# Moving 32 of a decoder layer's expert dot products from one stage to the next, with new layouts for two scratch tensors

## The chip, the cores and the metric

One core of a Trainium2 chip runs the whole kernel. The metric is the device time of one execution in microseconds (us), median of several runs. Five engines work side by side: TensorE (PE: matrix products), VectorE (DVE), ScalarE (ACT), GpSimd (POOL) and SyncE (SP, which here only issues transfers). They meet through semaphores. Transfers issued by SP share one queue, fetches of rows by index are issued by POOL on another; the same 16 transfer engines serve both.

## What is computed

The kernel is one layer of a decoder trunk for 512 tokens of 1024 channels; the change touches its last part, the PEER expert mixer with 16384 experts of one neuron each:

```python
def peer_ffn(h, w_q, sub_keys, u_experts, v_experts):
    ...                       # queries, scores, top 16 of each of 8 heads
    idx = ...                 # (tokens, 8, 16): 128 experts for each token
    g = jax.nn.softmax(best_s, axis=-1)
    act = jax.nn.gelu(jnp.einsum('cd,chkd->chk', xc, u_experts[ic]), approximate=False)
    wgt = gc * act
    return jnp.einsum('chk,chkd->cd', wgt, v_experts[ic])
```

The result is x + gate2 * peer_ffn(h2), followed by a last RMS norm.

## The kernel before

The expert mixer does not fetch rows for 384 of the 512 tokens. It computes the activation of all 16384 experts for them with TensorE, in 128 tiles of 128 experts (`phase_experts`), each with 24 matmuls in split precision: operands are cut into a high part (ACT) and a low part (POOL here), and three products are summed. The Gelu of each tile (ACT, L1647) goes to a DRAM tensor `acts`, two tiles at a time (`store`). Tiles 0 to 79 are "plain": DVE transposes their rows (L1714). Tiles 80 to 127 are "gated": their rows were turned in earlier stages and are loaded from DRAM (`load_turned`, L1594); beside them a dense table of gates for tokens and experts is built from one-hot products (DVE L1838 and L1842, 24 small matmuls of PE, ACT's copies L1685) and stored in 12 chunks of 32 tokens, 2 MB each (`gates_out`, L1589), one for every four tiles.

The first 128 tokens take the other way, by fetched rows. For each of their 128 choices (`NSLOT`) POOL fetches one row of `u_experts` for each token, 128 rows of 1024 channels (`fetch`, L1314), and DVE multiplies it with h, held in PSUM as `p_h`, and sums (`dot`, L1701). There are 4 buffers (`RING`). Which tile each dot stands beside is written out by hand: `dots_by(t)` puts 56 before tile 80 and the other 72 in the 48 gated tiles; `rows_by(t)` lets POOL run 4 ahead. On POOL the fetches stand behind the low part of each tile (L1857).

`phase_combine` multiplies activations with gates and with `v_experts`, in 32 groups of 4 tiles (`GT`), 72 matmuls of 512 columns each. For each group SP loads the activations (`at`, 768 KB), the gates (`gt`, 768 KB) and four tiles of values (`v`, 512 KB each, one buffer each, loaded again when its low part is done). DVE multiplies activations with gates (L2052, or L2074 in four pieces for group 0), takes low parts of values (L2046) and weights (L2057), ACT takes high parts (L2019, L2023). Between groups DVE adds fetched rows of `v_experts` for the first 128 tokens (`add_row`, L2067), 128 over 31 groups (`adds_by`), with 8 buffers (`VRING`). Each stage is a block; a block begins when all engines and the awaited stores of the last one are done. The values of group 0 and its activations are loaded before the end of `phase_experts`, its gates at the start of `phase_combine`.

Of the kernel before, what the change touches and what calls it, by code (L numbers as in the profile page):

```python
# [1316 lines left out]
def expert_groups(a, acts):  # L1317

    return a["v_experts"][0].rearrange("(g x p) d -> g p x d", x=GT, p=P), acts.rearrange("(g x) p t -> g p x t", x=GT)
# [192 lines left out]

def rows_by(t):

    return 0 if t < KNOWN_AT else min(NSLOT, dots_by(t + 1 if t + 1 < PLAIN else t) + RING)


def phase_experts(nc, a, keep, scores, top, topi, acts, gates, turned, raw, u_in, v, at0, v_in, w_in0, rows, few):

    with ExitStack() as stack:  # L1520
# [13 lines left out]
        gs = [k.sb(f"gs{j}", [P, P, CH]) for j in range(2)]  # L1534
        end = k.at
# [19 lines left out]
        iota = k.sb("iota", [P, P], BF16)  # L1555
        assert k.at <= TOP_AT
        k.at = TOP_AT
        parts = k.sb("parts", [P, NT // GTOK, 3, GTOK, 2], BF16)
        assert k.at <= V_AT
# [9 lines left out]
        au = acts.rearrange("(b x) p t -> b p x t", x=2)  # L1569
# [8 lines left out]
        def _(sp):  # L1578
# [4 lines left out]
            def store(n, j):  # L1583
                sp.wait_ge(sem["act_ok"], 2 * n + 2)
                sp.dma_start(au[n], ao[j][:, :, :]).then_inc(sem[f"a_out{j}"], 16)
# [10 lines left out]
            with sp.Fori(0, PLAIN // 4 - 1) as i:  # L1596
                for j in range(2):
                    load(2 * i + j + 2, j)
                    store(2 * i + j, j)
            for j in range(2):  # L1600
                sp.wait_ge(sem["ut_ok"], PLAIN - 2 + 2 * j)
                load_turned(j, j)
                store(PLAIN // 2 - 2 + j, j)

            def turn(i, last=False):
                for x in range(UNROLL // 2):
# [6 lines left out]
                    store(n, x % 2)  # L1613
                    if last and x == UNROLL // 2 - 2:
# [79 lines left out]
        def _(dve):  # L1694
# [108 lines left out]
            assert tile[0] <= SOFT_AT + 2  # L1803
            for t in range(tile[0], SOFT_AT + 2):
# [127 lines left out]

def adds_by(g):

    return NSLOT * g // (NE // P // GT - 1)


def phase_combine(nc, a, keep, acts, gates, gate2_row, x2, out, v, at0, v_in, w_in0, rows, few):

    with ExitStack() as stack:  # L1940
# [3 lines left out]
        at1 = k.sb("at1", [P, GT, NT])  # L1944
        at = [at0, at1]
        gt = [k.sb(f"gt{j}", [P, CHUNKS, GT * CH]) for j in range(2)]
        ssq, fin, root = (k.sb(n, [P, TT]) for n in ("ssq", "fin", "root"))
        assert k.at <= AT0_AT
        k.at = Y_AT + 48 * KB
        w_hi = [k.sb(f"w_hi{j}", [P, GT, NT], F32R) for j in range(2)]  # L1950
        w_lo = [k.sb(f"w_lo{j}", [P, GT, NT], F32R) for j in range(2)]
        gate2 = k.sb("gate2", [P, D])
        g_fin = k.sb("g_fin", [P, D])
# [12 lines left out]
        names = ("w_in1 w0_ok hi0_ok gf_in vhi_ok vlo_ok w_ok whi_ok wlo_ok mm "  # L1966
# [7 lines left out]
        gv = gates.rearrange("c j (g x) t -> g j c (x t)", x=GT)  # L1974
# [3 lines left out]
        def _(sp):  # L1978
# [5 lines left out]
            def weights(g, j):  # L1984
                sp.dma_start(at[j][:, :, :], av[g]).then_inc(sem[f"w_in{j}"], 16)
                sp.dma_start(gt[j][:, :, :], gv[g]).then_inc(sem[f"w_in{j}"], 16)
# [18 lines left out]
        def _(pool):  # L2005
            for n in range(NSLOT):
                if n >= VRING:
                    pool.wait_ge(sem["add_ok"], n - VRING + 1)
                gather_rows(nc, ring[n % VRING], a["v_experts"], few["idx"], n).then_inc(row_in[n % VRING], 16)

        @block.scalar
        def _(act):
# [16 lines left out]
            nc.scalar.activation(few["dots"][:, :], few["dots"][:, :], ACT.Gelu).then_inc(sem["dg_ok"], 1)  # L2029
            split(1, 1, True)  # L2030
            weights(1, 1)
            with act.Fori(1, NG // 2) as i:
# [9 lines left out]
        def _(dve):  # L2042
# [5 lines left out]
            def weigh(g):  # L2048
                j = g % 2
                dve.wait_ge(sem[f"w_in{j}"], 32 * (g // 2) + 32)  # L2050
                x = at[j][:, :, :].rearrange("p x (c t) -> p x c t", t=CH)
                nc.vector.tensor_tensor(x, x, gt[j][:, :, :].rearrange("p c (x t) -> p x c t", t=CH), ALU.mult).then_inc(sem["w_ok"], 1)  # L2052
# [6 lines left out]
            def add_row(n):  # L2059

                dve.wait_ge(row_in[n % VRING], 16 * (n // VRING) + 16)
                w = few["wg"][:, n:n + 1]
                if n == 0:
                    nc.vector.tensor_scalar(p_a[:, :], ring[0], w, None, ALU.mult).then_inc(sem["add_ok"], 1)
# [175 lines left out]
```

## Time and profile before

| what | value |
|---|---|
| median of 3 runs | 2024.35 us (2022.98 to 2035.23) |
| the profiled execution, its own time | 2025.17 us |
| its span, first to last instruction | 2023.3 us |
| PE / DVE / ACT / POOL busy | 1868 / 1498 / 721 / 781 us |
| expert tiles, last matmul | 1469.2 us |
| combine, first matmul | 1487.2 us |
| mean granted TensorE clock | 0.965 |

The span is the time from the first to the last instruction of the profiled execution; 1.9 us of its own time lie outside. Busy time is a share of the whole kernel and says little of a stage: a stage has to be read from windows, and its end from what the engines wait for. PEclk is the share of full clock (2.4 GHz) that TensorE was granted, DMA share the mean busy share of the 16 transfer engines as the profile counts it (it can come out above 1), GB/s what they moved.

### The profile page before, as it was taken

The numbers are of one execution on the slowest core, as the hardware profiler recorded it, in microseconds if no ns is written. First come the engines' busy times: TensorE is split into PE (matmuls) and PEld (weight loads), VectorE is DVE, ScalarE is ACT, GpSimd is POOL, SyncE is SP. The second block draws the span as 40 slices with busy tenths as digits, with TensorE's granted clock in tenths as the row PEclk, the third lists the DMA queues.
The fourth block names the chain that finished last, engine by engine and source line by source line (L and its number), as shares of the span: only waits on it lengthen the run. The fifth ranks groups of instructions, "written<-read, shape, count | busy, mean of one in ns | idle before, by whom it ended". The sixth has DMA issues, their size and how long they took to land. (4 is left out here: it accounts for less than half of the span.)

```text
span 2023.3 us, 28278 instructions
## 1 busy us (share of the span) xinstructions
PE 1868.2 (92%) x10096; PEld 1632.8 (81%) x10096; DVE 1497.6 (74%) x2260; ACT 720.6 (36%) x969; POOL 780.8 (39%) x487
## 2 busy tenths in 40 slices
PE   4999979999898799989999998999969999999997
PEld 4788757777777688989999988898858888888886
DVE  6566377774446488999895688888858887888887
ACT  3222234444323222323333354555533333333331
POOL 0000096000041001568787787888622332322320
PEclk7999989999999899999999999999979999999999
DMA  8799288878582431669999989999999999999991
GB/s 294 239 334 319 93 214 225 242 215 244 170 277 42 93 77 35 157 177 268 294 268 287 270 256 311 313 316 319 331 361 381 383 384 366 363 355 354 362 352 64
DMA packets 325795, 526.33 MB, mean 260 GB/s; under 512 B 20266, under 2 KB 243291, under 8 KB 321116
## 3 DMA queue, kind: packets, MB, share of 16 engines
q1 hardware_dynamic: 288860, 391.23, 64.2%
q0 software_dynamic: 36864, 134.23, 19.4%
q8 instruction: 34, 0.56, 0.1%
q14 instruction: 37, 0.30, 0.0%
HBM read 438.88 MB, written 85.99 MB: 259 GB/s over the span
## 5 line engine op out<-in xcount | busy, mean ns | idle before, releaser
L123 PE MATMUL u_s<-h_hi,u_hi 128*128 128x384 f32 x1024 | 358.1, 350 | 46.3 <-POOL u_lo L1857 41.6
L124 PE MATMUL u_s<-h_lo,u_hi 128*128 128x384 f32 x1024 | 348.8, 341 | 0.0
L125 PE MATMUL u_s<-h_hi,u_lo 128*128 128x384 f32 x1024 | 348.8, 341 | 0.0
L123 PE MATMUL v_o<-v_v_hi,v_w_hi 128*128 128x512 f32 x768 | 299.9, 391 | 18.7 <-DVE v_w_lo L2080 18.0
L124 PE MATMUL v_o<-v_v_lo,v_w_hi 128*128 128x512 f32 x768 | 299.7, 390 | 0.0
L125 PE MATMUL v_o<-v_v_hi,v_w_lo 128*128 128x512 f32 x768 | 299.5, 390 | 0.0
L2019 ACT ACTIVATE v_v_hi<-v_raw 128x1024 fp32r<-128x1024 f32 x128 | 127.7, 1053 | 340.0 <-PE v_o L125 268.3
L123 PEld LDWEIGHTS u_s<-h_hi,u_hi 128*128 128x128 f32 x1024 | 197.0, 192 | 59.6 <-POOL u_lo L1857 39.4
L1857 POOL TENSOR_TENSOR u_lo<-u_ut,u_hi 128x1024 fp32r<-128x1024 f32 x79 | 198.4, 2511 | 89.2 <-ACT u_hi L1635 89.1
L2046 DVE TENSOR_TENSOR v_v_lo<-v_raw,v_v_hi 128x1024 fp32r<-128x1024 f32 x128 | 149.4, 1221 | 87.8 <-ACT v_v_hi L2019 87.5
L124 PEld LDWEIGHTS u_s<-h_lo,u_hi 128*128 128x128 f32 x1024 | 197.2, 193 | 0.0
L125 PEld LDWEIGHTS u_s<-h_hi,u_lo 128*128 128x128 f32 x1024 | 197.0, 192 | 0.0
L1701 DVE CUSTOM_DVE_ANT_0 rows_buf<-rows_buf,u_h 128x1024 f32<-128x1024 f32 x128 | 154.2, 1210 | 45.8 <-DMA rows_buf<-in_u_experts_dram,few_idx 45.6
L123 PEld LDWEIGHTS v_o<-v_v_hi,v_w_hi 128*128 128x128 f32 x768 | 144.7, 188 | 49.4 <-issue 19.4
L1314 POOL DMA_INDIRECT rows_buf<-in_u_experts_dram,few_idx x128 | 169.2, 1322 | 36.3 <-DVE few_dots L1701 16.6
L1647 ACT ACTIVATE u_ao<-u_s 128x384 f32<-128x384 f32 x128 | 63.3, 494 | 326.7 <-PE u_s L125 309.5
L125 PEld LDWEIGHTS v_o<-v_v_hi,v_w_lo 128*128 128x128 f32 x768 | 144.7, 188 | 30.3
L124 PEld LDWEIGHTS v_o<-v_v_lo,v_w_hi 128*128 128x128 f32 x768 | 144.7, 188 | 30.0
L1314 POOL DMA_INDIRECT rows_buf<-in_v_experts_dram,few_idx x64 | 80.7, 1261 | 185.6 <-DVE v_a L2067 148.5
L1857 POOL TENSOR_TENSOR u_lo<-u_raw,u_hi 128x1024 fp32r<-128x1024 f32 x48 | 136.0, 2834 | 39.7 <-ACT u_hi L1640 39.0
L1314 POOL DMA_INDIRECT v_acc<-in_v_experts_dram,few_idx x64 | 78.4, 1225 | 167.4 <-DVE v_a L2067 164.4
L1714 DVE STREAM_TRANSPOSE u_ut<-u_raw 128x1024 f32<-128x1024 f32 x80 | 99.4, 1242 | 47.9 <-DMA u_raw<-in_u_experts_dram 47.5
(313 smaller groups left out, 3803.0 us busy)
## 6 DMA issues: line engine op xcount, KB each, us to landing
v_raw<-in_v_experts_dram SPq DMA_DIRECT2D x128, 512.0 KB
u_raw<-in_u_experts_dram SPq DMA_DIRECT2D x160, 256.0 KB
expert_acts<-u_ao SPq DMA_DIRECT2D x64, 384.0 KB
u_raw<-turned_experts SPq DMA_DIRECT2D x96, 256.0 KB
expert_gates<-u_gs SPq DMA_DIRECT2D x12, 2048.0 KB, 12.0
v_gt<-expert_gates SPq DMA_DIRECT2D x32, 768.0 KB
w_in_raw<-in_w_in_dram SPq DMA_DIRECT2D x17, 1024.0 KB, 11.7
proj_ada<-in_w_ada_dram SPq DMA_DIRECT2D x8, 2048.0 KB, 13.1
```

What stands on the lines that cost most here:

```text
L123: nc.tensor.matmul(out, w[0], x[0], start=first, stop=False)
L124: nc.tensor.matmul(out, w[0], x[1], start=False, stop=False)
L125: return nc.tensor.matmul(out, w[1], x[0], start=False, stop=last)
L1314: return nc.gpsimd.indirect_dma_start(to, None, table[0], bass.IndirectOffsetOnAxis(idx[:, n:n + 1], 0))
L1647: nc.scalar.activation(ao[j // 2][:, j % 2, :], p_s[j % 2][:, 0:NT], ACT.Gelu).then_inc(sem["act_ok"], 1)
L1701: nc.vector.tensor_tensor_reduce(out=row, in0=row, in1=p_h[:, :], scale=1.0, scalar=0.0, op0=ALU.mult, op1=ALU.add, accum_out=few["dots"][ ...
L1714: nc.vector.transpose(ut[j % 2][:, :, :].rearrange("p m (b e) -> p b m e", b=4), half.rearrange("p b (m r) -> p b m r", m=KD)).then_inc(se ...
L1857: nc.gpsimd.tensor_tensor(lo[j][:, :, :], ut[j][:, :, :] if t < PLAIN else at_half(t % 4), hi[j][:, :, :].bitcast(F32), ALU.subtract).then ...
L2019: nc.scalar.activation(v_hi[j][:, x, :], v[:, x, :], ACT.Copy).then_inc(sem["vhi_ok"], 1)
L2046: nc.vector.tensor_tensor(v_lo[g % 2][:, x, :], v[:, x, :], v_hi[g % 2][:, x, :].bitcast(F32), ALU.subtract).then_inc(sem["vlo_ok"], 1)
```

## The change

- `dots_by` puts 46 dots into the plain tiles and 50 into the gated ones (`SOON`, 96 in all). The other 32 (`LATE`) are done in the combine: two a group in groups 1 to 16, ahead of the rows of `v_experts`. All 160 row steps are spread evenly over the 31 groups. For them h is copied from PSUM to SBUF (`ht`) at the end of the plain tiles, and ACT does a second Gelu after group 17, whose product with the gates DVE takes after group 19.
- `acts` is laid out as [32 groups, 128, 4, 384] instead of [128 tiles, 128, 384]. The stores are still of two tiles; a load of a group is one contiguous piece in each partition.
- Gates are loaded for two groups at a time from group 2 on (`gate_pair`), pieces of 1024 bytes instead of 512, and up to two groups ahead.
- The first group's gates are loaded at the end of `phase_experts`, eleven of twelve chunks (`gt0`); the twelfth is read where it was computed (`gs[1]`). Its multiplication is in eight pieces instead of four.
- The first two tiles of group 0's values are loaded as soon as their buffer is free, and not with the other two. `g_fin` and `gate2`, used at the end, are loaded at the end instead of behind group 1. Some buffers change place for this; SP's and ACT's loops are written out or split.

```diff
-    ... acts.rearrange("(g x) p t -> g x p t", x=GT)
+    ... acts
-DOTS_FROM, EARLY_DOTS = 22, 56
+DOTS_FROM, EARLY_DOTS = 22, 46
+LATE = 32
+SOON = NSLOT - LATE
+LATE_BY = 16
...
-    return EARLY_DOTS + (NSLOT - EARLY_DOTS) * (t + 1 - PLAIN) // GATED
+    return EARLY_DOTS + (SOON - EARLY_DOTS) * (t + 1 - PLAIN) // GATED
...
+def gates_of(gates, n):
+
+    return gates.rearrange("c j (g x) t -> g j c (x t)", x=n)
...
                         sp.dma_start(at0[:, :, :], av[0]).then_inc(w_in0, 16)
-                        sp.wait_ge(sem["lo_ok"], TILES)
+                        for y in range(2):
+                            sp.wait_ge(sem[f"g_out{y}"], 16 * (TURNS - y))
+                        sp.dma_start(gt0[:, 0:CHUNKS - 1, :], gates_of(gates, GT)[0][:, 0:CHUNKS - 1, :]).then_inc(w_in0, 16)
                         for y in range(GT):
+                            if y % 2 == 0:
+                                sp.wait_ge(sem["lo_ok"], TILES - 2 + y)
                             sp.dma_start(v[:, y, :], vv[0][:, y, :]).then_inc(v_in[y], 16)
...
+            dve.wait_ge(sem["ht_ok"], 2)
+            dve.wait_ge(steps.sem, steps.n)
+            nc.vector.tensor_copy(ht[:, :], p_h[:, :])
...
+def late_by(g):
+
+    return LATE * min(g, LATE_BY) // LATE_BY
...
-    return NSLOT * g // (NE // P // GT - 1)
+    return (NSLOT + LATE) * g // (NE // P // GT - 1) - late_by(g)
...
-            sp.dma_start(gt[0][:, :, :], gv[0]).then_inc(sem["w_in0"], 16)
-            weights(1, 1)
+            def gate_pair(i):
+                sp.dma_start(gt[i % 2][:, :, :, :].rearrange("p c y n -> p c (y n)"), gv[i]).then_inc(sem[f"gt_in{i % 2}"], 16)
+
+            sp.dma_start(gt[0][:, :, 1, :], gv1).then_inc(sem["gt_in0"], 16)
+            weights(1)
             values(1)
+            gate_pair(1)
+            for g in range(2, NG):
+                if g % 2 == 0 and g + 2 < NG:
+                    sp.wait_ge(sem["w_ok"], g - 1)
+                    gate_pair(g // 2 + 1)
+                sp.wait_ge(sem["wlo_ok"], g - 1)
+                weights(g)
+                values(g)
+            sp.wait_ge(sem["w_ok"], NG - 3)
             sp.dma_start(g_fin[:, :], ...)
             sp.dma_start(gate2[:, :], ...)
-            with sp.Fori(1, NG // 2) as i:
-                for j in range(2):
-                    sp.wait_ge(sem["wlo_ok"], 2 * i + j - 1)
-                    weights(2 * i + j, j)
-                    values(2 * i + j)
...
+            act.wait_ge(sem["add_ok"], LATE + adds_by(LATE_BY - 1))
+            nc.scalar.activation(few["dots"][:, SOON:], few["dots"][:, SOON:], ACT.Gelu).then_inc(sem["dg_ok"], 1)
...
+            def late_dot(at_row, n):
+
+                dve.wait_ge(row_in[at_row % VRING], 16 * (at_row // VRING) + 16)
+                row = ring[at_row % VRING]
+                nc.vector.tensor_tensor_reduce(out=row, in0=row, in1=ht[:, :], scale=1.0, scalar=0.0, op0=ALU.mult, op1=ALU.add,
+                                               accum_out=few["dots"][:, late_slot(n):late_slot(n) + 1]).then_inc(sem["add_ok"], 1)
...
-                    o = at[0][:, x, :].rearrange("p (c t) -> p c t", t=CH)
-                    nc.vector.tensor_tensor(o, o, gt[0][:, :, x * CH:(x + 1) * CH], ALU.mult).then_inc(sem["w0_ok"], 1)
+                    o = at[0][:, x, 0:NT - CH].rearrange("p (c t) -> p c t", t=CH)
+                    nc.vector.tensor_tensor(o, o, gt0[:, 0:CHUNKS - 1, x * CH:(x + 1) * CH], ALU.mult)
+                    o = at[0][:, x, NT - CH:]
+                    nc.vector.tensor_tensor(o, o, gs[1][:, x, :], ALU.mult).then_inc(sem["w0_ok"], 1)
...
                 if g == 1:
                     dve.wait_ge(sem["wg_ok"], 1)
+                for n in range(late_by(g - 1), late_by(g)):
+                    late_dot(at_row, n)
+                    at_row += 1
                 for n in range(adds_by(g - 1), adds_by(g)):
-                    add_row(n)
+                    add_row(at_row, n)
+                    at_row += 1
+                if g == LATE_BY + 3:
+                    dve.wait_ge(sem["dg_ok"], 2)
+                    nc.vector.tensor_tensor(few["wg"][:, SOON:], few["dots"][:, SOON:], sel[:, 2, 0, SOON:], ALU.mult).then_inc(sem["wg_ok"], 1)
+                    dve.wait_ge(sem["wg_ok"], 2)
...
-        acts = nc.dram_tensor("expert_acts", [NE // P, P, NT], F32, kind="Internal").ap()
+        acts = nc.dram_tensor("expert_acts", [NE // P // GT, P, GT, NT], F32, kind="Internal").ap()
```

## Rows read from the trace of the kernel before

**Rows 1.** Windows: length, busy times, PEclk, DMA share, GB/s

```profile
891.00:1165.00 274.00, 261.13 (x1458) 252.16 (x1458) 220.94 (x496) 92.13 (x125) 211.46 (x121) 0.99 1.02 273
1165.00:1205.00 40.00, 40.00 (x348) 38.65 (x348) 36.82 (x36) 23.10 (x27) 36.49 (x17) 1.00 0.87 258
1205.00:1469.00 264.00, 239.58 (x1959) 231.29 (x1956) 214.05 (x202) 137.66 (x163) 202.56 (x99) 0.95 1.03 317
1520.00:1600.00 80.00, 80.00 (x354) 66.24 (x354) 70.39 (x54) 29.06 (x26) 25.64 (x21) 1.00 1.06 380
1700.00:1900.00 200.00, 200.00 (x884) 165.60 (x883) 160.06 (x124) 64.69 (x62) 64.02 (x51) 1.00 1.01 359
```

**Rows 2.** Timeline of ACT: start, length, instruction, idle before and its releaser

```profile
1268.23 0.49 ACT L1647 ACTIVATE u_ao<-u_s 128x384 f32<-128x384 f32 x1 [1.48 <-PE u_s L125]
...
1284.97 0.49 ACT L1647 ACTIVATE u_ao<-u_s 128x384 f32<-128x384 f32 x1 [2.17 <-PE u_s L125]
...
1294.17 0.53 ACT L1647 ACTIVATE u_ao<-u_s 128x384 f32<-128x384 f32 x1
```

**Rows 3.** Waits from 1165 to 1470 us: total, times, longest

```profile
DVE rows_buf L1701 <- DMA rows_buf<-in_u_experts_dram,few_idx: 45.6, 27, 4.7
ACT u_hi L1640 <- DMA u_raw<-turned_experts: 44.9, 12, 6.5
...
PE u_s L123 <- POOL u_lo L1857: 23.0, 8, 7.0
```

**Rows 4.** Windows of two microseconds in the gated tiles, same columns

```profile
1264.00:1266.00 2.00, 2.00 (x13) 2.00 (x13) 1.97 (x3) 2.00 (x3) 1.99 (x2) 1.00 1.00 208
1276.00:1278.00 2.00, 2.00 (x14) 2.00 (x13) 1.48 (x1) 1.40 (x2) 1.98 (x2) 1.00 1.04 442
```

**Rows 5.** Timeline of DVE, steady part of the combine

```profile
1764.57 1.75 DVE L2052 TENSOR_TENSOR at_raw<-at_raw,v_gt 128x1536 f32<-128x1536 f32 x1
1769.31 4.63 DVE L2046 TENSOR_TENSOR v_v_lo<-v_raw,v_v_hi 128x1024 fp32r<-128x1024 f32 x4 [2.98 <-ACT v_v_hi L2019]
...
1775.52 2.68 DVE L2067 SCALAR_TENSOR_TENSOR v_a<-v_acc,few_wg,v_a 128x1024 f32<-128x1024 f32 x2
...
1780.89 1.75 DVE L2052 TENSOR_TENSOR v_at<-v_at,v_gt 128x1536 f32<-128x1536 f32 x1
```

**Rows 6.** Timeline of DVE and of ACT, early in the combine

```profile
1573.17 1.75 DVE L2052 TENSOR_TENSOR at_raw<-at_raw,v_gt 128x1536 f32<-128x1536 f32 x1
...
1588.25 1.75 DVE L2052 TENSOR_TENSOR v_at<-v_at,v_gt 128x1536 f32<-128x1536 f32 x1
...
1572.72 2.26 ACT L2019 ACTIVATE v_v_hi<-v_raw 128x1024 fp32r<-128x1024 f32 x2 [6.62 <-DMA v_raw<-in_v_experts_dram]
```

**Rows 7.** The page's costliest groups: busy us and mean ns of one

```profile
L1701 DVE CUSTOM_DVE_ANT_0 rows_buf<-rows_buf,u_h 128x1024 f32<-128x1024 f32 x128 | 154.2, 1210 | 45.8 <-DMA rows_buf<-in_u_experts_dram,few_idx 45.6
...
L1314 POOL DMA_INDIRECT rows_buf<-in_u_experts_dram,few_idx x128 | 169.2, 1322 | 36.3 <-DVE few_dots L1701 16.6
```

**Rows 8.** Timeline of DVE, end of the plain tiles

```profile
1144.81 0.69 DVE L1808 TENSOR_REDUCE u_z<-few_sel 128x32 f32<-128x512 f32 x1 [4.70 <-ACT few_sel L1665]
```

**Rows 9.** Windows of four microseconds early in the combine

```profile
1566.00:1570.00 4.00, 4.00 (x19) 3.30 (x19) 3.77 (x3) 0.09 (x1) 0.65 (x1) 1.00 1.13 331
1570.00:1574.00 4.00, 4.00 (x20) 3.30 (x19) 3.79 (x4) 1.16 (x2) 2.64 (x4) 1.00 1.03 405
```

**Rows 10.** Timeline of SP, DVE and PE at the change of stage

```profile
1466.45 0.34 SPq L1589 DMA_DIRECT2D expert_gates<-u_gs  x1
...
1482.81 1.02 DVE L2074 TENSOR_TENSOR at_raw<-at_raw,v_gt 128x384 f32<-128x384 f32 x2
...
1497.32 1.76 DVE L2052 TENSOR_TENSOR v_at<-v_at,v_gt 128x1536 f32<-128x1536 f32 x1 [10.06 <-DMA v_gt<-expert_gates]
...
1487.21 0.77 PE L123 MATMUL v_o<-v_v_hi,v_w_hi 128*128 128x512 f32 x1 [18.02 <-DVE v_w_lo L2080]
```

**Rows 11.** Timeline of DVE at the end of the kernel

```profile
2002.13 1.23 DVE L2095 TENSOR_TENSOR v_acc<-v_o,v_gate 128x1024 f32<-128x1024 f32 x1 [3.49 <-PE v_o L125]
```

More of the change, by code:

```diff
@@ L1509, in dots_by, with phase_experts @@
         return EARLY_DOTS * max(0, t + 1 - DOTS_FROM) // plain
-    return EARLY_DOTS + (NSLOT - EARLY_DOTS) * (t + 1 - PLAIN) // GATED
+    return EARLY_DOTS + (SOON - EARLY_DOTS) * (t + 1 - PLAIN) // GATED
 def rows_by(t):
-    return 0 if t < KNOWN_AT else min(NSLOT, dots_by(t + 1 if t + 1 < PLAIN else t) + RING)
-def phase_experts(nc, a, keep, scores, top, topi, acts, gates, turned, raw, u_in, v, at0, v_in, w_in0, rows, few):
+    return 0 if t < KNOWN_AT else min(SOON, dots_by(t + 1 if t + 1 < PLAIN else t) + RING)
+def gates_of(gates, n):
+    return gates.rearrange("c j (g x) t -> g j c (x t)", x=n)
+def phase_experts(nc, a, keep, scores, top, topi, acts, gates, turned, raw, u_in, v, at0, gt0, gs, ht, v_in, w_in0, rows, few):
     with ExitStack() as stack:
@@ L1533, in phase_experts @@
         gs_at = k.at
-        gs = [k.sb(f"gs{j}", [P, P, CH]) for j in range(2)]
-        end = k.at
+        end = gs_at + 32 * KB
         k.at = gs_at
@@ L1598, in _ @@
                     load(2 * i + j + 2, j)
-                    store(2 * i + j, j)
+                    store(i, j)
             for j in range(2):
@@ L1930, with late_slot, phase_combine @@
 VRING = 8
+def late_by(g):
+    return LATE * min(g, LATE_BY) // LATE_BY
 def adds_by(g):
-    return NSLOT * g // (NE // P // GT - 1)
-def phase_combine(nc, a, keep, acts, gates, gate2_row, x2, out, v, at0, v_in, w_in0, rows, few):
+    return (NSLOT + LATE) * g // (NE // P // GT - 1) - late_by(g)
+def late_slot(n):
+    return SOON + n
+def phase_combine(nc, a, keep, acts, gates, gate2_row, x2, out, v, at0, gt0, gs, ht, v_in, w_in0, rows, few):
     with ExitStack() as stack:
@@ L2005, in _ @@
         def _(pool):
[L2006 to L2009, printed above, removed]
+            at_row = 0
+            for g in range(1, NG):
+                for n in range(late_by(g - 1), late_by(g)):
+                    if at_row >= VRING:
+                        pool.wait_ge(sem["add_ok"], at_row - VRING + 1)
+                    gather_rows(nc, ring[at_row % VRING], a["u_experts"], few["idx"], late_slot(n)).then_inc(row_in[at_row % VRING], 16)
+                    at_row += 1
+                for n in range(adds_by(g - 1), adds_by(g)):
+                    if at_row >= VRING:
+                        pool.wait_ge(sem["add_ok"], at_row - VRING + 1)
+                    gather_rows(nc, ring[at_row % VRING], a["v_experts"], few["idx"], n).then_inc(row_in[at_row % VRING], 16)
+                    at_row += 1
         @block.scalar
@@ L2028, in _ @@
                 nc.scalar.activation(w_hi[0][:, x, :], at[0][:, x, :], ACT.Copy).then_inc(sem["hi0_ok"] if x < GT - 1 else sem["whi_ok"], 1)
-            nc.scalar.activation(few["dots"][:, :], few["dots"][:, :], ACT.Gelu).then_inc(sem["dg_ok"], 1)
+            nc.scalar.activation(few["dots"][:, 0:SOON], few["dots"][:, 0:SOON], ACT.Gelu).then_inc(sem["dg_ok"], 1)
             split(1, 1, True)
             weights(1, 1)
-            with act.Fori(1, NG // 2) as i:
+            with act.Fori(1, LATE_BY // 2 + 1) as i:
+                for j in range(2):
+                    split(2 * i + j, j)
+                    weights(2 * i + j, j)
+            act.wait_ge(sem["add_ok"], LATE + adds_by(LATE_BY - 1))
+            nc.scalar.activation(few["dots"][:, SOON:], few["dots"][:, SOON:], ACT.Gelu).then_inc(sem["dg_ok"], 1)
+            with act.Fori(LATE_BY // 2 + 1, NG // 2) as i:
                 for j in range(2):
@@ L2082, in _ @@
             dve.wait_ge(sem["dg_ok"], 1)
-            nc.vector.tensor_tensor(few["wg"][:, :], few["dots"][:, :], sel[:, 2, 0, :], ALU.mult).then_inc(sem["wg_ok"], 1)
+            nc.vector.tensor_tensor(few["wg"][:, 0:SOON], few["dots"][:, 0:SOON], sel[:, 2, 0, 0:SOON], ALU.mult).then_inc(sem["wg_ok"], 1)
+            at_row = 0
             for g in range(1, NG):
```

72 lines of the change are left out of this document (38 added, 34 removed).

## The prediction

> **What bounds the kernel now.** Read the stages first, in the windows [rows 1]. From 891 to 1469 us (expert tiles) TensorE has idle time; from 1520 us on (combine) it has none. So time can come back from the expert tiles and the change of stage, and the combine can only lose some.
>
> The expert tiles first. ACT's Gelu marks the end of each tile: from 1268.23 to 1284.97 three tiles pass, 5.58 us each [rows 2]. That is TensorE's own period there (24 small and 24 large matmuls). The next end comes at 1294.17, 9.20 us later. The windows count this: 1165 to 1205 holds 348 matmuls, 7.25 tiles of 48, in 40 us, 5.5 us each; 1205 to 1469 holds 1959, 40.8 tiles in 264 us, 6.47 us each, at a mean granted clock of 0.95 of the 2.4 GHz level [rows 1]. The later part is (6.47 - 5.58) x 40.8 = 36 us over TensorE's own pace. That is the largest thing to be had.
>
> What ends those waits [rows 3]: ACT waits 44.9 us for the load of turned rows (12 times, up to 6.5 us), DVE 45.6 us for fetched rows, and TensorE, behind both, for POOL's low part. The transfer engines are busy all the time (share 1.03) at only 317 GB/s, against a share of 0.87 and no idle TensorE before 1205 [rows 1]. Two-microsecond windows show why the rate is low: 208 GB/s while turned rows are loaded, 442 at another time, both at a full share [rows 4]. So this part is short of transfer time, with POOL not far behind: 202.6 us busy over 40.8 tiles is 4.96 of 5.58 us.
>
> In the combine TensorE needs 16.32 us a group: DVE's weighing (L2052) starts at 1764.57 and 1780.89, with 2.98 us of idle DVE in between, waiting for TensorE by way of ACT [rows 5]. Early on the same line starts at 1573.17 and 1588.25 [rows 6]: 15.08 us with four rows added. That is quicker than TensorE, because the stage began about a group late and is catching up, and it is limited by transfers, since ACT waits for v_raw, 6.62 us in that row. These are the two bounds of the combine: TensorE 16.32, transfers 15.08 with four rows.
>
> **The change, part by part.**
>
> *Fewer dots beside the gated tiles.* 128 dots become 96: 56 to 46 in the plain tiles, 72 to 50 in the 48 gated ones, which is 1.50 to 1.04 a tile. Each is a 512 KB transfer, 1.32 us of POOL and 1.21 us of DVE [rows 7]. A row's price in transfer time lies between 0.524 MB / 442 GB/s = 1.19 us and 0.524 / 208 = 2.5 us [rows 4]. For 0.46 row a tile that is 0.55 to 1.15 us. The present 6.47 us would fall to 5.3 to 5.9, and TensorE stops it at 5.58. POOL falls to 4.96 - 0.46 x 1.32 = 4.35 us. I take 5.85 us: near the low price, because transfers remain nearly full, and a gate store of 2 MB every fourth tile still stands ahead of a turned load on SP's queue. Gain (6.47 - 5.85) x 40.8 = 25 us; bounds 12 us (half of the cheaper price, the rest lost in bursts) and 36 us (5.58).
>
> *The ten dots taken from the plain tiles.* TensorE idles 274 - 261 = 13 us there [rows 1], at a full share of the transfer engines. Ten of 56 dots less takes a sixth of the row traffic away: I take 3 us, between 0 and 8. The copy of the first tokens' h to SBUF is one DVE instruction of 1024 columns from PSUM, about the 1.21 us of a dot; it goes between the signal `picked` and the sum that waits 4.70 us for ACT's exponentials, which hides it [rows 8]. Without that cover it would cost 1.2 us.
>
> *Activations in groups of four tiles.* The stores keep count and bytes; a partition's piece grows from 1536 to 3072 bytes, and the loads go from four pieces of 1536 to one of 6144. No row separates the sizes there; 0 to 0.2 us a group, in favour; I take 0.
>
> *Gates by two groups.* In the combine's transfer-limited stretch four microseconds of each period run slower than the next four [rows 9]: 331 against 405 GB/s. I read the dip as the gate load with its 512-byte pieces, issued behind the activations. Four microseconds at 331 instead of 405 GB/s is 0.7 us a group; pieces of 1024 bytes should return half, 0.35 us, bounds 0 and 0.7. The Trainium skill, page "DMA: Bandwidth & Descriptors", section Specifications, says that 512 bytes are enough for the full rate; by that the regrouping would return nothing. The dip speaks against it, though its cause is my reading.
>
> *The row work in the combine.* 128 rows over 31 groups become 160, 4.13 to 5.16 a group. DVE: from 1775.52 to 1780.89 four rows take 5.37 us, 1.34 each [rows 5]; its work of 16.32 - 2.98 = 13.34 us becomes 14.9 on average and 16.0 with six rows, still under 16.32, and 1.4 of the 2.98 idle us are left. Transfers: 15.08 us with four rows, 5.77 MB at 383 GB/s, gets 1.16 rows x 1.3 us (0.524 MB at 405 GB/s) = 1.5 and loses 0.35: 16.25 us. That is just under TensorE's 16.32. So in the steady part nothing is lost, but the lead that the old kernel built in its first hundred microseconds (1.25 us a group) now grows slowly, and in every second group a 1.5 MB gate load stands ahead of the values. I charge 2 us, bounds 0 and (16.6 - 16.32) x 31 = 9 us. The second Gelu, its product and the two added waits meet work that ended a group before: nothing.
>
> *The change of stage.* TensorE stops at 1469.2 and starts at 1487.21. The last gate store is issued at 1466.45 and the next block's first product (L2074) starts at 1482.81 [rows 10]. The first gates now come before that store, 0.72 MB, 1.8 us at 405 GB/s, on a full queue, with about one row fewer. In return the first gate load leaves the new block; but L2074 shows no wait before it, it starts when the four low parts end: the gates were not what the path waited for. The four products become eight. Two of 384 columns take 1.02 us [rows 10]; one of 32 columns lies between its share, 0.04, and 0.3, and the first four shrink by a twelfth: +0.5 us in all. Splitting the loads of v gives the first two about 2 us earlier. Net I take +1 us, from -2 to +3. Group 1 had DVE waiting 10.06 us for its gates [rows 10]; with one load and the two final rows (1 MB) out of its way they come some 2 us earlier, which pays a part of the slower start.
>
> *The end.* Group 31 gets six rows instead of five, 1.3 us; before the output of the second token block DVE idles 3.49 us for TensorE [rows 11], so nothing.
>
> Sum against the profiled execution, 2025.17 us (span 2023.3 plus 1.9 outside): -25 - 3 + 2 + 1 = -25, 2000.2. The median of the runs shown is 0.8 us lower; I say **2000 us**.
>
> **The rivals.**
> A. *The bursts stay.* What makes turned loads late may be the gate store ahead of them in one queue, not the number of rows. For it: ACT's waits are few and long, and the windows at 208 GB/s are not those of row fetches. Against: POOL and DVE wait as well. Gated gain 10, the rest -3 + 2 + 1: 2015.
> B. *The gated part reaches TensorE's pace.* For it: before 1205, at share 0.87, TensorE has no idle time, and 0.46 row less frees at least 0.55 of 6.47 us. 36 us there, 6 in the plain part: 2025 - 42 + 2 = 1985.
> C. *The combine turns transfer-limited* in part: pieces of 1024 bytes bring nothing and each even group comes late. The 9 us of the bound and 1 of start on the forecast: 2010.
> D. *The added rows cost the combine more than they free*, the slower case. Where transfers collide, a row's price was up to 2.5 us. The combine's period is then 15.08 + 1.16 x 2.5 = 18.0, and 31 x 1.7 = 52 us are lost: 2000 + 50 = 2050. It decides from the price at which 31 groups lose 25 us, (16.32 + 0.8 - 15.08) / 1.16 = 1.76 us a row. Against it: 4.13 rows already ride at 380 GB/s [rows 1]. The Trainium skill, page "DMA: Bandwidth & Descriptors", section Bandwidth, gives about 358 GB/s as the memory's limit for a core; 6.38 MB a group by that is 17.8 us, the same end. The window of 380 GB/s over 80 us lies above it, so the trace disagrees and I give it little.
>
> **How the numbers follow.** Forecast 0.52 (its own range 1992 to 2008), A 0.20, B 0.14, C 0.10, D 0.04. The range must leave out no more than two in ten and takes in B and A: 1984 to 2021. A measurement of this kernel tells about 1% from no change, 20 us. Faster (below 2004): three quarters of the forecast, all of B, some of C: 0.56. Slower (above 2044.6): D, 0.04. Within 1%: 0.40.
>
> **What would show it.** In the new profile: gated tiles 5.6 to 5.9 us apart on average, ACT's wait for turned rows well under 44.9 us, the granted clock there above 0.95; in the combine 16.32 us a group, DVE idle 1.4 us in each instead of 2.98, rates near 390 GB/s and TensorE waits of 0 to 3 us in the first groups; 17 to 20 us between the stages with DVE's first product again without a wait. I am wrong if the gated bursts keep their number and length, or if TensorE waits in the combine beyond 1600 us.

## The result and the profile after

The changed kernel takes 2040.93 us (median of 20 runs, 2029.41 to 2048.42), the kernel before 2028.83 us (20 runs, 2021.56 to 2035.23): 1.0063 of the time before, 95% interval 1.0048 to 1.0078. It is slower by 0.6%, and the forecast was 1.2% faster. The profiled execution took 2041.97 us, with a span of 2040.2.

The windows of the changed kernel, against [rows 1] (columns as there; the gated part ends earlier now, so the third window is cut at 1435):

```profile
891.00:1165.00 274.00, 262.54 (x1465) 253.83 (x1464) 213.86 (x477) 91.70 (x125) 202.51 (x111) 0.99 0.97 254
1165.00:1205.00 40.00, 40.00 (x353) 38.90 (x354) 39.73 (x32) 23.15 (x27) 34.49 (x15) 1.00 0.87 245
1205.00:1435.00 230.00, 227.70 (x1951) 220.89 (x1948) 215.87 (x163) 140.04 (x162) 177.15 (x78) 1.00 1.01 315
1520.00:1600.00 80.00, 75.59 (x325) 61.69 (x324) 61.40 (x56) 24.82 (x22) 25.67 (x21) 0.98 0.93 346
1700.00:1900.00 200.00, 187.18 (x799) 152.73 (x798) 162.27 (x131) 66.72 (x60) 67.83 (x58) 0.97 0.96 359
```

The gated part gained more than forecast. Its window before 1205 looks as it did; after that 1951 matmuls, 40.6 tiles, stand in 230 us, 5.66 us each, where [rows 1] had 6.47. Of the 33 us, 22 are idle time of TensorE that is gone (2.3 us are left of 24.4); the other 11 are matmuls that run faster, at a granted clock of 1.00 instead of 0.95. The combine lost: from 1700 to 1900 TensorE executes 799 matmuls and is busy 187.2 us, where [rows 1] had 883 or 884 and 200. And the transfer engines, full before with 359 GB/s, move the same 359 GB/s at a share of only 0.96, although each group has half a megabyte more to load.

ACT's Gelu at the ends of gated tiles, against [rows 2], is nearly regular, 5.57 us from one to the next in the last two rows and within 0.1 of 5.58 in 35 of the 48 tiles:

```profile
1209.83 0.49 ACT L1656 ACTIVATE u_ao<-u_s 128x384 f32<-128x384 f32 x1 [0.94 <-PE u_s L125]
...
1226.57 0.49 ACT L1656 ACTIVATE u_ao<-u_s 128x384 f32<-128x384 f32 x1 [2.13 <-PE u_s L125]
...
1232.14 0.49 ACT L1656 ACTIVATE u_ao<-u_s 128x384 f32<-128x384 f32 x1
```

and the wait for turned rows has fallen from 44.9 us [rows 3] to

```profile
ACT u_hi L1649 <- DMA u_raw<-turned_experts: 12.1, 10, 2.4
```

(total, times, longest). The last matmul of the expert tiles starts at 1435.6 us instead of 1468.9: 33 us gained. Such starts are what "the expert tiles end" means below.

The combine's TensorE work, from the start of its first matmul to that of its last product of two high parts (L123), runs from 1456.5 to 2027.7 us, 571 us, where it took 525 (1487.2 to 2012.1): 46 us lost. The combine is measured like this in every run below. The whole stage in one window, after and before:

```profile
1456.50:2028.50 572.00, 539.02 (x2304) 440.43 (x2304) 464.79 (x402) 177.27 (x159) 182.77 (x154) 0.97 0.92 343
```

```profile
1487.20:2013.00 525.80, 525.04 (x2304) 433.93 (x2304) 425.09 (x339) 168.63 (x159) 151.21 (x123) 1.00 0.95 343
```

So 32 of the 46 us are idle time, and 14 are the same 2304 matmuls running longer, at a mean granted clock of 0.97.

DVE's weighing of the groups, against [rows 5], is no longer even:

```profile
1720.06 1.75 DVE L2095 TENSOR_TENSOR v_at<-v_at,v_gt 128x1536 f32<-128x1536 f32 x1
...
1735.00 1.76 DVE L2095 TENSOR_TENSOR at_raw<-at_raw,v_gt 128x1536 f32<-128x1536 f32 x1 [0.51 <-DMA at_raw<-expert_acts]
...
1755.83 1.75 DVE L2095 TENSOR_TENSOR v_at<-v_at,v_gt 128x1536 f32<-128x1536 f32 x1
```

From an odd group (1720.06) to the even one behind it (1735.00) pass 14.94 us, and from there to the next odd one (1755.83) 20.83: 35.8 us for two groups, where TensorE needs 32.6. In the 13 pairs that lie wholly in the stage's even part they are 34.3 to 37.1 us. The waits of the stage show for what, and this time TensorE waits too:

```profile
ACT v_v_hi L2054 <- DMA v_raw<-in_v_experts_dram: 292.8, 99, 21.9
...
PE v_o L123 <- DVE v_w_lo L2100: 33.0, 13, 5.8
```

ACT waits 293 us for the values in 99 waits. Before the change it waited mostly for TensorE, and 63.7 us for values:

```profile
ACT v_v_hi L2019 <- PE v_o L125: 268.3, 25, 11.0
```

Ten of TensorE's 13 waits come later than 1600 us, which the prediction had named as a sign of being wrong. After some of them the granted clock falls from 2.4 to 1.2 GHz; here the next matmul follows after 0.55 us, and those behind it every 0.43, where 0.23 is usual:

```profile
1749.51 0.76 PE L123 MATMUL v_o<-v_v_hi,v_w_hi 128*128 128x512 f32 x1 [2.83 <-DVE v_w_lo L2100]
1750.06 0.63 PE L124 MATMUL v_o<-v_v_lo,v_w_hi 128*128 128x512 f32 x1
1750.49 0.63 PE L125 MATMUL v_o<-v_v_hi,v_w_lo 128*128 128x512 f32 x1
```

SP's issues around one even group, and under them ACT's first high part of its values:

```profile
1721.84 0.38 SPq L2009 DMA_DIRECT2D v_gt<-expert_gates  x1
1722.26 3.26 SPq L2006 DMA_DIRECT2D at_raw<-expert_acts  x1
1725.57 2.46 SPq L2003 DMA_DIRECT2D v_raw<-in_v_experts_dram  x4
1728.08 0.48 SPq L2006 DMA_DIRECT2D v_at<-expert_acts  x1
1739.98 7.92 SPq L2003 DMA_DIRECT2D v_raw<-in_v_experts_dram  x4
1757.61 0.38 SPq L2009 DMA_DIRECT2D v_gt<-expert_gates  x1
...
1737.63 1.06 ACT L2054 ACTIVATE v_v_hi<-v_raw 128x1024 fp32r<-128x1024 f32 x1 [14.29 <-DMA v_raw<-in_v_experts_dram]
```

DVE weighs the odd group at 1720.06. Only then SP may load the next pair of gates (1.5 MB), since it goes over the gates just used. Behind it follow the even group's activations, whose issue takes 3.26 us behind the gates, and from 1725.57 its values. ACT gets the first of these at 1737.63, 17.6 us after the weighing. At the start of that stretch and behind its end the transfers move less than in between. Three windows of the same two groups:

```profile
1722.00:1728.00 6.00, 6.00 (x28) 4.96 (x27) 6.00 (x6) 1.34 (x1) 0.63 (x1) 1.00 0.93 294
1734.00:1748.00 14.00, 12.67 (x56) 10.14 (x55) 7.46 (x7) 5.61 (x5) 3.27 (x2) 1.00 1.03 411
1750.00:1754.00 4.00, 4.00 (x13) 3.13 (x12) 3.79 (x6) 3.54 (x4) 2.61 (x2) 0.63 0.55 172
```

While the gates come first, 294 GB/s; while the activations and values come in, 411; behind the last values, 172 GB/s at a share of 0.55. SP's last issue ended at 1747.90, it stands at the wait for the next weighing (1755.83), and until 1757.61 it sends nothing; only row fetches go on. So the transfers come in one lump of some 28 us in a pair of groups, followed by a gap, and the values of the even group come late in the lump.

The gap of TensorE between the stages grew from 18.02 us [rows 10] to 20.54:

```profile
1456.51 0.76 PE L123 MATMUL v_o<-v_v_hi,v_w_hi 128*128 128x512 f32 x1 [20.54 <-DVE v_w_lo L2132]
```

### The profile page after: what moved, and what is told of

Read it like the earlier page. It is cut to its first block and busy times, and to the rows that moved or that the text cites. A ratio compares the mean times of both kernels' runs of the same rounds, so it can differ in the third digit from the quotient of the medians.

```text
span 2040.2 us, 27828 instructions
## 1 busy us (share of the span) xinstructions
PE 1873.8 (92%) x10096; PEld 1633.5 (80%) x10096; DVE 1535.2 (75%) x2266; ACT 731.4 (36%) x970; POOL 775.0 (38%) x487
## 5 line engine op out<-in xcount | busy, mean ns | idle before, releaser
L123 PE MATMUL u_s<-h_hi,u_hi 128*128 128x384 f32 x1024 | 354.6, 346 | 24.1 <-POOL u_lo L1869 19.1
L123 PE MATMUL v_o<-v_v_hi,v_w_hi 128*128 128x512 f32 x768 | 306.1, 399 | 53.5 <-DVE v_w_lo L2100 33.0
L124 PE MATMUL v_o<-v_v_lo,v_w_hi 128*128 128x512 f32 x768 | 304.0, 396 | 0.0
L125 PE MATMUL v_o<-v_v_hi,v_w_lo 128*128 128x512 f32 x768 | 303.7, 395 | 0.0
L2054 ACT ACTIVATE v_v_hi<-v_raw 128x1024 fp32r<-128x1024 f32 x128 | 134.7, 1059 | 335.6 <-DMA v_raw<-in_v_experts_dram 293.4
L123 PEld LDWEIGHTS u_s<-h_hi,u_hi 128*128 128x128 f32 x1024 | 194.5, 190 | 35.8 <-POOL u_lo L1869 25.6
L123 PEld LDWEIGHTS v_o<-v_v_hi,v_w_hi 128*128 128x128 f32 x768 | 147.3, 192 | 90.2 <-DVE v_w_lo L2100 38.7
L1314 POOL DMA_INDIRECT rows_buf<-in_u_experts_dram,few_idx x111 | 148.9, 1342 | 44.5 <-POOLq L1528 17.8
L1142 POOL TENSOR_TENSOR gate_merged<-gate_merged,gate_part 128x512 f32<-128x512 f32 x24 | 33.4, 1408 | 246.6 <-DVE gate_part L1107 246.6
```

The costliest lines, as they stand in the source:

```text
L123: nc.tensor.matmul(out, w[0], x[0], start=first, stop=False)
L124: nc.tensor.matmul(out, w[0], x[1], start=False, stop=False)
L125: return nc.tensor.matmul(out, w[1], x[0], start=False, stop=last)
L1142: nc.gpsimd.tensor_tensor(merged[:, c, :], merged[:, c, :], part[m][:, :], ALU.add).then_inc(sem["add_ok"], 1)
L1314: return nc.gpsimd.indirect_dma_start(to, None, table[0], bass.IndirectOffsetOnAxis(idx[:, n:n + 1], 0))
L2054: nc.scalar.activation(v_hi[j][:, x, :], v[:, x, :], ACT.Copy).then_inc(sem["vhi_ok"], 1)
```

## The experiments

Two theories stood at the start. **Order:** the pair of gates, tied to a wait and put ahead of the even group's activations and values on SP's queue, makes these late. **Rows:** 5.16 row steps a group are simply more than transfers or DVE can carry beside TensorE (rival D of the prediction, and C in part). Each kernel was timed against the kernel before on the same chip; the ratio stands with its 95% interval.

### 1. The pair of gates behind the values

```diff
             for g in range(2, NG):
-                if g % 2 == 0 and g + 2 < NG:
-                    sp.wait_ge(sem["w_ok"], g - 1)
-                    gate_pair(g // 2 + 1)
                 sp.wait_ge(sem["wlo_ok"], g - 1)
                 weights(g)
                 values(g)
+                if g % 2 == 0 and g + 2 < NG:
+                    sp.wait_ge(sem["w_ok"], g - 1)
+                    gate_pair(g // 2 + 1)
```

> The changed kernel, with the load of a pair of gates issued behind the activations and values of its even group instead of ahead of them; bytes, rows and waits stay. Theory 1 (order): in the combine SP stands at the wait for DVE's weighing (w_ok) with the activations and values of the even group behind it, and then sends 1.5 MB of gates ahead of them on the same queue. By it the pair of groups (35.6 us now) falls to two times TensorE's 16.32, the combine loses about 40 us, total near 2000, and ACT's waits for v_raw (293 us) fall under 100. Theory 2 (rows): 5.16 rows a group are too much for the transfers or DVE; by it the order changes nothing, total stays near 2040.

Measured: 1994.29 us, 0.9808 (0.9783 to 0.9832). TensorE's combine runs from 1458.3 to 1982.5 us, 524.2 us: all of the 46 us is back by moving three lines of SP's order, with the same bytes, the same rows, the same pieces. Windows, then waits, of this kernel:

```profile
1520.00:1600.00 80.00, 80.00 (x355) 66.24 (x354) 71.22 (x66) 25.45 (x23) 32.98 (x26) 1.00 1.03 403
...
1700.00:1900.00 200.00, 200.00 (x884) 165.62 (x883) 179.49 (x143) 63.75 (x61) 78.86 (x67) 1.00 1.03 397
```

```profile
ACT v_v_hi L2054 <- PE v_o L125: 240.8, 25, 11.0
ACT v_v_hi L2054 <- DMA v_raw<-in_v_experts_dram: 85.3, 32, 12.0
```

TensorE is never idle in the windows, and the transfers move 403 and 397 GB/s, beside 346 and 359 in the changed kernel. SP's issues around an even group:

```profile
1628.47 4.06 SPq L2003 DMA_DIRECT2D v_raw<-in_v_experts_dram  x4
1632.57 0.43 SPq L2009 DMA_DIRECT2D v_gt<-expert_gates  x1
1634.11 10.48 SPq L2006 DMA_DIRECT2D v_at<-expert_acts  x1
1644.63 2.91 SPq L2003 DMA_DIRECT2D v_raw<-in_v_experts_dram  x4
```

The issue that now gets stuck behind the gates is that of the next, odd group's activations, 10.48 us. They are not needed before that group's weighing. The rows theory falls.

### 2. The pair behind the activations, ahead of the values

```diff
-                if g % 2 == 0 and g + 2 < NG: (wait and gate_pair)
                 sp.wait_ge(sem["wlo_ok"], g - 1)
                 weights(g)
+                if g % 2 == 0 and g + 2 < NG: (wait and gate_pair)
                 values(g)
```

> The changed kernel, with only the activations of the even group moved ahead of the wait and of the pair of gates; the values stay behind them. Theory 1 (order): splits it in two. The values were in any case issued right after the weighing, so what is undone is the 0.75 MB of activations (about 2 us of queue) and the stretch in which the queue runs empty before the weighing; 1.5 MB of gates still stand ahead of the values. I expect a third to a half of the loss back, pairs of groups near 34 us, total 2010 to 2025. Theory 2 (rows): unchanged, 2040.

Measured: 2002.34 us, 0.9852 (0.9825 to 0.9880), faster than I expected. The combine takes 531.6 us. Of the 47 us between the changed kernel and experiment 1, the even group's activations ahead of the gates account for 39.6 and its values for 7.4. Of these 7.4, 5.0 are the one wait of TensorE, which ends at 1497.37:

```profile
PE v_o L123 <- DVE v_w_lo L2100: 5.0, 1, 5.0
```

In the steady part gates between the weighing and the values cost TensorE no wait. The activations can be sent as soon as the low part of the weights is done, six row steps before the weighing; I read that as the work which fills the gap in the queue; experiment 5 tests it.

### 3. Without the late dots in the combine

```diff
-                for n in range(late_by(g - 1), late_by(g)):   (POOL's fetches and DVE's dots)
-    return (NSLOT + LATE) * g // (NE // P // GT - 1) - late_by(g)
+    return NSLOT * g // (NE // P // GT - 1)
```

> The changed kernel without the 32 late dots and their fetches in the combine: these 32 weights are left out of the computation (their sums get other numbers, Gelu and product stay), 128 row steps over 31 groups as in the kernel before. Theory 2 (rows): the combine returns to 16.32 us a group, total near 1995. Theory 1 (order): the long wait for values in every even group stays; only 0.5 MB of 6.4 goes and DVE's 1.3 us a group, so the pair of groups falls from 35.6 by 1.5 to 3 us, total 1995 to 2020 with waits for v_raw of more than 10 us in every even group. The length of the even groups' waits decides.

This kernel leaves the 32 late dots out of the computation. Measured: 2020.52 us, 0.9930 (0.9905 to 0.9955), at the upper end of what the order theory gave. With the old number of rows the combine still takes 546.1 us (1463.4 to 2009.5), 21 more than before the change, and ACT's wait for values is nearly what it was:

```profile
ACT v_v_hi L2050 <- DMA v_raw<-in_v_experts_dram: 265.1, 80, 20.6
```

The rows make the lump longer: without 32 of them it costs 21 us instead of 46. They don't make it.

### 4. Gates for one group at a time

```diff
+            def gate_one(g):
+                sp.dma_start(gt[g % 2][:, :, :], gv[g]).then_inc(sem[f"gt_in{g % 2}"], 16)
...
-                if g % 2 == 0 and g + 2 < NG: (wait and gate_pair)
                 sp.wait_ge(sem["wlo_ok"], g - 1)
                 weights(g)
+                gate_one(g)
                 values(g)
```

> The changed kernel with gates loaded for one group at a time in pieces of 512 bytes, behind the activations and ahead of the values as in the kernel before, no wait for the weighing; rows, layout of the activations and the prefetch stay. Theory 1 (order): the alternation of short and long groups goes, TensorE's 16.32 us a group or, limited by transfers, 16.6; total 1995 to 2010. Theory 2 (rows): 5.16 rows stay, so 18 us a group stays, total near 2040.

Measured: 1999.08 us, 0.9826 (0.9800 to 0.9852). The combine takes 523.4 us, as in experiment 1, but with ACT waiting 327 us for values (107 waits, and none for TensorE): it is limited by transfers all the way, just at TensorE's pace. The profiled execution was the slowest of four (2005.33). Window from 1700 to 1900:

```profile
1700.00:1900.00 200.00, 200.00 (x884) 165.59 (x883) 177.41 (x141) 68.73 (x63) 75.19 (x62) 1.00 1.05 391
```

391 GB/s with gates in pieces of 512 bytes, 397 to 403 with 1024. 391 GB/s is also what TensorE's pace asks for, 6.38 MB in 16.32 us; that it is the limit here is read from ACT's waits, which go on to the end.

### 5. The wait without the bytes

```diff
                 if g % 2 == 0 and g + 2 < NG:
                     sp.wait_ge(sem["w_ok"], g - 1)
-                    gate_pair(g // 2 + 1)
                 sp.wait_ge(sem["wlo_ok"], g - 1)
                 weights(g)
                 values(g)
+                if g % 2 == 0 and g + 2 < NG:
+                    gate_pair(g // 2 + 1)
```

> The changed kernel with only the wait for DVE's weighing left ahead of the even group's activations; the load of a pair of gates itself goes behind the values. Of the order theory it separates the wait from the bytes. Theory 1a (the wait): SP stands at the wait while the queue runs empty, and the activations and values go out too late whatever precedes them: total 2015 to 2035, long waits for v_raw in even groups stay. Theory 1b (the bytes): 1.5 MB of gates on the queue ahead of the others is what makes them late; with them behind, total 1994 to 2002.

Measured: 1994.49 us, 0.9844 (0.9804 to 0.9884); combine 523.7 us. The weighing of an odd group runs from 1622.01 to 1623.76; SP's issues behind it, and the window from 1700 to 1900:

```profile
1623.79 0.33 SPq L2006 DMA_DIRECT2D at_raw<-expert_acts  x1
1624.92 4.02 SPq L2003 DMA_DIRECT2D v_raw<-in_v_experts_dram  x4
1629.32 0.38 SPq L2009 DMA_DIRECT2D v_gt<-expert_gates  x1
```

```profile
1700.00:1900.00 200.00, 200.00 (x884) 165.69 (x883) 178.06 (x140) 66.03 (x64) 77.14 (x64) 1.00 1.03 398
```

So holding the activations back until the weighing costs nothing by itself. It is the 1.5 MB that must not stand between the weighing and the group it delays. When the gates go last, they fill the stretch that was empty. So of the two readings of the order theory the one by the wait falls and the one by the bytes holds. My reading of experiment 2 falls too, that early activations fill the gap: what counts is that gates and activations don't both come between the weighing and the values.

### 6. The new layouts without the move of the dots

Experiment 1 with `LATE = 0` and `EARLY_DOTS = 56`; the second Gelu and its product are gone with it.

> The kernel of the first experiment (pair behind the values) with all 128 dots back beside the expert tiles (56 and 72), none in the combine. It tests what shortened the gated tiles. If it was the 22 fetched rows and dots less: gated tiles are 6.3 to 6.5 us apart again, total 2022 to 2032. If it was the layout of the activations or the order at the end: they stay at 5.6 to 5.7 us and the total at 1990 to 2000.

Measured: 2034.86 us, 1.0031 (1.0001 to 1.0061). The expert tiles end at 1476.9 us and the combine takes 524.5. Waits from 1165 to 1430 us:

```profile
DVE rows_buf L1710 <- DMA rows_buf<-in_u_experts_dram,few_idx: 53.3, 22, 4.4
POOL rows_buf L1314 <- DVE few_dots L1710: 38.5, 20, 3.7
ACT u_hi L1649 <- DMA u_raw<-turned_experts: 21.5, 11, 3.9
```

DVE again waits for fetched rows and POOL for DVE. The gated part's gain comes from the dots. The layouts alone gain nothing; the time is a little above the 2022 to 2032 expected. Its expert tiles end 8 us later than those of the kernel before. That may be scatter: in the single traces of the changed kernel and of experiments 1, 2, 4, 5 and 12, whose expert tiles run the same program, they end between 1434.2 and 1444.5 us.

### 7. Activations tile by tile, as before

Experiment 1 with `acts` as [128, 128, 384].

> The kernel of the first experiment with the activations stored tile by tile as before (pieces of 1536 bytes both ways). The prediction charged 0 to 0.2 us a group. If that is right: 1994 to 1998, gated tiles and groups at the same pace. If small pieces load the queues more than that: transfers in the combine fall behind TensorE, 2000 or more.

Measured: 1997.30 us, 0.9847 (0.9808 to 0.9886), no difference in time that the intervals tell. The combine takes 524.1 us. Window from 1700 to 1900:

```profile
1700.00:1900.00 200.00, 200.00 (x884) 165.62 (x883) 178.25 (x143) 69.63 (x65) 75.41 (x63) 1.00 1.04 396
```

In the transfer-limited window from 1600 to 1700 it moved 396 GB/s where experiment 1 moved 402: for 6.38 MB a group 0.24 us.

### 8. First gates loaded in the combine

Experiment 1 with the load of `gt0` moved from the end of `phase_experts` to the start of `phase_combine`.

> The kernel of the first experiment with the first group's gates loaded at the start of the combine instead of the end of the expert tiles. The prediction says that this load was hidden behind the high and low parts of the values: the gap of TensorE between the stages (20.1 us there) falls to 17.5 to 19, since the last gate store leaves earlier, total 1992 to 1995. The rival: now nothing hides it, the gap grows by 2 to 5 us, 1996 to 2000.

Measured: 1996.74 us, 0.9846 (0.9808 to 0.9884). First matmul of the combine, in experiment 1 and here:

```profile
1458.26 0.77 PE L123 MATMUL v_o<-v_v_hi,v_w_hi 128*128 128x512 f32 x1 [20.14 <-DVE v_w_lo L2132]
```

```profile
1457.02 0.77 PE L123 MATMUL v_o<-v_v_hi,v_w_hi 128*128 128x512 f32 x1 [17.31 <-DVE v_w_lo L2130]
```

The gap is 2.8 us shorter without the prefetch, as predicted; but TensorE then waits 2.7 us once in the first groups, which it doesn't in experiment 1, and the combine takes 3.2 us more. The time is not the 1992 to 1995 expected. In sum the place of this load is worth nothing that can be measured.

### 9, 10. Sixteen and forty-eight late dots

Experiment 1 with `LATE, EARLY_DOTS` = 16, 51 and 48, 41.

> The kernel of the first experiment with 16 late dots instead of 32 (51 beside the plain tiles, 61 beside the gated ones: 1.27 a tile). The gated tiles took 6.37 us with 1.50 and 5.64 with 1.04. If a row has one price in transfer time, the middle is 6.0 us and the total 2008 to 2014. If the gated tiles are free from some point on (TensorE's pace reached as soon as POOL and the loads stay ahead), they are near 5.6 us already and the total is 1990 to 1998.

> The kernel of the first experiment with 48 late dots (41 and 39: 0.81 a gated tile; 176 row steps in the combine, 5.68 a group). The gated tiles stand at TensorE's pace already and gain at most 2 us. In the combine the transfers needed about 16.0 us a group with 5.16 rows; with 5.68 at 1.3 us each 16.7, over TensorE's 16.32: 10 us lost, total 2002 to 2008, and ACT waits for v_raw to the end. If the rows still fit, 1992 to 1996.

Measured: 2014.45 us, 0.9926 (0.9903 to 0.9948) with 16, and 2009.90 us, 0.9904 (0.9880 to 0.9927) with 48. The expert tiles end at 1476.9 us with no late dots (experiment 6), at 1464.2 with 16, 1437.8 with 32 and 1436.6 with 48. The trace with 16 is of the slowest of its four executions (2021.13 us), and its plain tiles end 4 to 11 us later than the others', so the ends don't compare well. The gated tiles alone do: from ACT's last plain Gelu to its last gated one they take 6.51 us each with no dots moved (1165.0 to 1477.3), 6.08 with 16 (1172.8 to 1464.6), 5.70 with 32 (1164.5 to 1438.2) and 5.62 with 48 (1167.3 to 1437.0). The first two steps of 16 give 0.43 and 0.38 us, about the same, as if a row had one price; the third gives 0.08, because 5.58 is TensorE's pace. The ratios of the times agree: 1.0031, 0.9926 and, in experiment 12, 0.9846. The combine takes 523.7 us with 16, 524.2 with 32 and 533.8 with 48, which brings the time with 48 just above the 2002 to 2008 expected. With 48 ACT waits for values to the end:

```profile
ACT v_v_hi L2054 <- DMA v_raw<-in_v_experts_dram: 266.9, 96, 13.2
...
ACT v_v_hi L2054 <- PE v_o L125: 38.3, 6, 8.6
```

### 11. The move of the dots alone

Experiment 4 with activations tile by tile and the first gates loaded in the combine.

> The move of the 32 dots alone: gates for one group in 512-byte pieces, activations tile by tile, first gates loaded in the combine, as in the kernel before (the places of some buffers and the end of g_fin and gate2 stay as changed). By the order theory the move needs none of the new layouts: gated tiles near 5.65 us, combine within 10 us of TensorE's pace, total 1996 to 2006. If small pieces cost what the prediction said (0.35 us for gates, up to 0.2 for activations), the combine loses (16.6 - 16.32) x 31 = 9 us against the first experiment, so 2003.

Measured: 2007.16 us, 0.9887 (0.9863 to 0.9912), a little above the 1996 to 2006 expected. The expert tiles end at 1440.1 us, 29 earlier than before the change: the dots give that without any layout. The combine takes 530.7 us. Window from 1700 to 1900:

```profile
1700.00:1900.00 200.00, 196.20 (x857) 161.61 (x856) 175.55 (x139) 67.74 (x62) 75.43 (x62) 0.99 1.05 385
```

385 GB/s, 12 less than with both new layouts, and TensorE idles 3.8 of 200 us. Here the layouts are worth their place: once rows are added, 12 GB/s decide whether 6.38 MB fit under TensorE's 16.32 us (16.6 at 385, 15.9 at 402).

### 12. The first experiment again

> The kernel of the first experiment once more, beside the other two amounts of late dots on the same chip and in more rounds, as the best version so far: 1990 to 1998, 0.979 to 0.984 of the kernel before. If the first result was the chip's doing, it lies outside.

Measured: 1997.07 us, 0.9846 (0.9825 to 0.9868), the median of five runs: the time as expected, the ratio just above the 0.979 to 0.984 given. The best version is 1.5 to 1.9% faster than the kernel before, and 2.2% faster than the changed kernel (by the two ratios, 0.9846 / 1.0063).

## Why the prediction was wrong

The step that failed is a term in *The row work in the combine*: "in every second group a 1.5 MB gate load stands ahead of the values. I charge 2 us", with bounds of 0 and 9. I had seen the load and priced it as bytes in an average: 16.25 us of transfers under 16.32 of TensorE. The average was right. Experiment 1 moves the same bytes, and in its transfer-limited stretch (18 groups from 1514.2 to 1802.3 us) a group takes 16.0 us. But an average holds only if the queue always has something to send. The order made it send 1.5 MB of gates, activations and values in one lump after the weighing, 17.6 us with the rows beside it until the first values are there, and then little until the next weighing. Cost: 46 us instead of 2, shown by experiments 1 and 5, in which the same load stands elsewhere. The prediction also had no price for what a wait does to the granted clock: 32 us of the 46 are TensorE's idle time, the other 14 its slower matmuls behind the waits.

Of waits the prediction names only "the two added waits" beside the second Gelu and its product. The wait for `w_ok` that SP got was not gone through for what is queued behind it. Experiment 5 shows that the wait alone is harmless; with the bytes at its side it fixes when the lump starts.

The other steps:
- *Gated tiles:* -25 us forecast (5.85 us a tile), 33 measured (5.66): rival B's size. The term was too small by 8 us, since I left residual bursts behind gate stores. Most of them went as the rows did; the gate store ahead of the loads, rival A's cause, stands there as before and does not make them by itself. B's own sum, 2025 - 42 + 2, leaves out the +1 of the change of stage.
- *Plain tiles:* -3 forecast, about 0 measured: 1465 matmuls from 891 to 1165 us instead of 1458, which is 0.3 tile, 1.3 us, and a first tile 1.3 us later.
- *Change of stage:* +1 forecast, +2.5 measured, and for the reason given: the last gate store stands behind the prefetched gates (experiment 8).
- *Gates by two groups:* 0.35 us a group forecast. From the rates, 6.38 MB at 391 and at 402 GB/s differ by 0.45 us (experiment 4).
- *Activations:* 0 to 0.2 us forecast, 0.24 measured (experiment 7).
- *A row's price in the combine:* 1.3 us forecast. From 5.16 to 5.68 rows the group went from 16.0 to 16.76 us (27 groups from 1514.0 to 1966.4 in experiment 10), 1.5 us a row. Rival D, with 2.5 us a row, had the sign of the result and the wrong cause. Rival C says that each even group comes late, which it does, but by the size of the gates' pieces, and priced it at 9 us.

With the order mended all these terms give -33 - 0 + 2.5 + 0 = -30.5 from 2025.17: 1994.7. Experiment 1 measures 1994.29, and its repetition 1997.07. That the first agrees within a microsecond is partly luck: against the kernel before on the same chip it is 37.3 us less, and the repetition 33.0.

One core moves 397 to 403 GB/s over 80 and 200 us in experiment 1. The Trainium skill, page "DMA: Bandwidth & Descriptors", section Bandwidth, has about 358 GB/s as a core's limit, and says beside its measured rates that this is the share when both cores of a pair stream and that a core alone moves more. Here one core runs the kernel, so the runs agree with the second statement; the prediction's 17.8 us a group took the share of a pair for the limit of a core alone. With gates in pieces of 512 instead of 1024 bytes, an eighth of the bytes (0.79 of 6.38 MB a group), the whole mix falls from 397 or 402 to 391 GB/s. The Trainium skill, the same page, section Specifications, says that 512 bytes are enough for the full rate; here they were not quite, as far as one pair of traces tells.

## What to carry to other kernels

When a transfer queue is nearly full on average, price a reordering by what stands between the event that frees a buffer and the load that is needed next, not by bytes per period; a big load that nobody needs yet belongs behind the small urgent ones, where it fills the time in which the queue would be empty. When a wait is added on an issuing engine, write down every transfer behind it and when each is needed. A wait of TensorE costs more than its length where the granted clock falls behind it: here 14 us on top of 32. And when a change in parts comes out slower, look whether its largest part has delivered: here 33 us were gained and 46 lost in another place, and moving three lines kept the first without the second.

## What the runs showed of the hardware

- An issue on SP's queue right behind a pair of gates (1.5 MB in pieces of 1024 bytes) is itself slow: 1.46 to 16.97 us for the 768 KB of activations in experiment 1, 10.48 in the rows above. The activations that are issued behind four loads of values (2 MB) take 0.33 us there. SP's later issues wait with a slow one, urgent or not.
- With one core, loads from memory and row fetches together sustained 397 to 403 GB/s at a share of 1.03. The gated part was at a full share with 317 GB/s before the change and with 312 in experiment 1 [rows 1]. A full share and a rate are two things, and what lowers the rate there (the turned rows, four loads of 32 partitions each, beside windows of 208 GB/s in [rows 4]) was not taken apart.
- TensorE's matmuls of 512 columns follow each other every 0.23 us at the 2.4 GHz level and every 0.43 at 1.2 GHz. In the changed kernel's combine the granted clock falls to the lower level behind six of the 13 waits. The waits' lengths don't sort them: one of 1.95 us (ending at 1533.24) had a fall behind it, one of 2.70 (1962.93) had none.
- The gated tiles' time falls by 0.43 and 0.38 us for each 16 dots moved, and by 0.08 for the third 16, once it is at TensorE's 5.58 us.
